# Moving 15 gathered rows from the last stretch of a PEER layer to its projections

## What is computed

```python
proj = rms_norm(x, norm_mix) @ w_in                # q, k, v, u_g, v_g
y = concat(rms_norm(stick_breaking_attention(q, k, v)), rms_norm(chunked_spatial_gating(u_g, v_g)))
x = x + y @ w_out
h2 = rms_norm(x, norm_ffn)
# PEER: product-key retrieval, 8 heads x 16 experts of 16384 for every token
q = rms_norm((h2 @ w_query).reshape(t, 8, 256)); s1, s2 = q halves @ sub_keys
expert_idx, gate = top 16 of the 16 x 16 sums of the two top-16 lists
u_sel = expert_u[expert_idx]                       # (t, 128, 2048)
act = gelu(einsum('tkd,td->tk', u_sel, h2)) * gate
x = x + einsum('tk,tkd->td', act, expert_v[expert_idx])
```

## Time and profile before

| | |
|---|---|
| median of 3 runs | 2982.95 us |
| the profiled execution's own time | 2975.43 us |
| its span, first to last instruction | 2973.7 us |
| busy: PE, DVE, ACT, POOL | 94%, 75%, 40%, 52% |
| mean granted TensorE clock | 0.97 of full speed |
| moved by DMA | 949.46 MB, mean 319 GB/s |
| rows (lines 1328 and 1341) | 208 and 205 instructions |

### The profile page before, as it was taken

How to read it: one execution, slowest core, us unless ns; L and a number is a source line. 1 busy time by engine, 2 the same in 40 slices (tenths; PEclk the granted TensorE clock), 3 DMA queues, 4 the chain that set the end, 5 groups by cost and what they waited for, 6 DMA issues and landing times.

```text
span 2973.7 us, 43212 instructions
## 1 busy us (share of the span) xinstructions
PE 2803.9 (94%) x17757; PEld 2643.4 (89%) x17757; DVE 2233.4 (75%) x3157; ACT 1181.3 (40%) x1387; POOL 1533.8 (52%) x664
## 2 busy tenths in 40 slices
PE   7899899988999989989999899999999999999998
PEld 6677788866879989989999899999999999999997
DVE  6756576766677789979997577777777777778786
ACT  6755532357323333333433333434333333333321
POOL 0000154222242367863334488888867777766662
PEclk9999999989999999999999899999999999999999
DMA  9737638863797868877789899999999999999995
GB/s 362 277 142 263 232 128 328 335 255 127 301 355 279 341 247 297 298 276 298 309 304 371 333 371 353 379 366 383 376 360 407 411 411 388 393 384 382 364 371 217
DMA packets 189485, 949.46 MB, mean 319 GB/s; under 512 B 18352, under 2 KB 77792, under 8 KB 79552
## 3 DMA queue, kind: packets, MB, share of 16 engines
q1 hardware_dynamic: 116704, 485.55, 43.5%
q0 software_dynamic: 60848, 440.59, 38.0%
q10 hardware_dynamic: 11808, 21.70, 1.9%
HBM read 906.46 MB, written 41.22 MB: 319 GB/s over the span
## 4 chain that ended last, share of the span: by engine, by line
PE 69%; DVE 11%; DMA 11%; ACT 5%; POOL 2%; issue 1%; SPq 1%; ACTq 0%; DVEq 0%
PE ps L1686 14%; PE ps L2034 8%; PE ps L2036 8%; PE ps L2035 8%; PE ps L1967 7%; PE ps L1965 6%; PE ps L1966 6%; PE ps L1950 4%; DVE ring_lo L1099 4%; PE ps L1673 4%; DMA ring_raw<-peer_v 3%; POOL ring_lo L617 2%; DVE ps L1341 2%; ACT ring_hi L689 2%; DVE hot_a L1535 2%
## 5 line engine op out<-in xcount | busy, mean ns | idle before, releaser
L617 POOL TENSOR_TENSOR ring_lo<-ring_raw,ring_hi 128x2048 fp32r<-128x2048 f32 x215 | 1000.1, 4652 | 701.5 <-ACT ring_hi L689 699.9
L689 ACT ACTIVATE ring_hi<-ring_raw 128x2048 fp32r<-128x2048 f32 x400 | 762.0, 1918 | 688.2 <-DMA ring_raw<-peer_u 222.8
L1965 PE MATMUL ps<-bT_hi,ring_hi 128*128 128x304 f32 x2048 | 629.3, 307 | 33.0 <-DVE ring_lo L1099 24.8
L2034 PE MATMUL ps<-a_hi,ring_hi 128*128 128x304 f32 x2048 | 629.3, 307 | 31.2 <-DVE ring_lo L1099 15.8
L2036 PE MATMUL ps<-a_hi,ring_lo 128*128 128x304 f32 x2048 | 624.7, 305 | 0.0
L1967 PE MATMUL ps<-bT_hi,ring_lo 128*128 128x304 f32 x2048 | 624.2, 305 | 0.0
L1966 PE MATMUL ps<-bT_lo,ring_hi 128*128 128x304 f32 x2048 | 623.3, 304 | 0.0
L2035 PE MATMUL ps<-a_lo,ring_hi 128*128 128x304 f32 x2048 | 621.8, 304 | 0.0
L1099 DVE TENSOR_TENSOR ring_lo<-ring_raw,ring_hi 128x2048 fp32r<-128x2048 f32 x185 | 452.6, 2462 | 174.9 <-ACT ring_hi L689 174.7
L1965 PEld LDWEIGHTS ps<-bT_hi,ring_hi 128*128 128x128 f32 x2048 | 392.5, 192 | 35.3 <-issue 30.2
L2034 PEld LDWEIGHTS ps<-a_hi,ring_hi 128*128 128x128 f32 x2048 | 390.8, 191 | 36.8 <-issue 27.2
(11 more groups left out here) (310 smaller groups left out, 3772.3 us busy)
## 6 DMA issues: line engine op xcount, KB each, us to landing
ring_raw<-peer_u SPq DMA_DIRECT2D x128, 1024.0 KB, 7.6
ring_raw<-peer_v SPq DMA_DIRECT2D x128, 1024.0 KB, 8.0
ring_raw<-w_in SPq DMA_DIRECT2D x80, 1024.0 KB, 5.4
ring_raw<-w_out SPq DMA_DIRECT2D x32, 1024.0 KB, 4.8
ring_raw<-w_query SPq DMA_DIRECT2D x32, 1024.0 KB, 6.5
g_pair<-gates_scratch SPq DMA_DIRECT2D x64, 320.0 KB, 8.8
gelu_scratch<-ahead ACTq DMA_DIRECT2D x72, 152.0 KB, 5.3
g_in<-gelu_scratch SPq DMA_DIRECT2D x72, 152.0 KB, 7.5
```

The source lines that it names most:

```text
L617: pool.tensor_tensor(ring_lo[s][:], ring_raw[s][:], ring_hi[s][:].bitcast(F32), ALU.subtract)\
L689: act.activation(ring_hi[place(n)][:], ring_raw[place(n)][:], ACT.Copy).then_inc(hi_ok[SLOT[n]], 1)
L1965: pe.matmul(dst, hi[:, e], bT_hi[:, k, 0:NEAR], start=(k == 0), stop=False)
L2034: pe.matmul(dst, hi[:, col], a_hi[:, par, e, :], start=(e == 0), stop=False)
```

## The change

Only the numbers in `fill_rows` change. Beside pieces 94, 98, 102, 106 and 110 of w_in, 115, 119 and 123 of w_out and 130, 132, 134, 136, 138, 140 and 142 of w_query DVE does one row more: two beside each piece of w_in and w_out up to 125, three beside every second piece of w_query. By AHEAD 120 rows are placed instead of 105. The numbers of AHEAD and DOWN stay, so their rows are others: each place there has the row 15 further on in the list. BOTH has 152 rows in place of 167, spread evenly over its 112 pieces (a pattern of 1, 1, 2 in place of 1, 2). Buffers, and which rows read h from SBUF, follow from the same functions.

```diff
 def fill_rows():
     for n in range(92, OUT_B):
-        ROWS_AT[n] = 1 if n % 4 == 2 else 2
+        ROWS_AT[n] = 2
     ROWS_AT[OUT_B - 1] += sum(ATTEND_ROWS)
     for n in range(OUT_B, AHEAD - 1):
-        ROWS_AT[n] = 0 if n == QUERY_B - 1 else 1 if n == QUERY_B - 2 or n % 4 == 3 and n < QUERY_B else 2
+        ROWS_AT[n] = 0 if n == QUERY_B - 1 else 1 if n == QUERY_B - 2 else 3 if n > QUERY_B and n % 2 == 0 else 2
     for t in range(3):
```

## The result

The changed kernel takes **2994.0 us** (median of 12 runs, 2983.16 to 3002.32) beside 2982.32 us of the kernel before on the same chip (12 runs, 2966.58 to 2997.83): a ratio of 1.0039, 95% interval 1.0023 to 1.0056. It is slower by 12 us, where 6.5 us less was forecast. The profiled execution took 2993.33 us (span 2991.6, granted clock 0.971), so it stands for the median; that of before lay 7.5 us under the median that the forecast started from.

What follows compares the result with a forecast made beforehand. PE was taken to bound the kernel nearly everywhere, the last stretch losing some 41 us. Terms -22 - 7.5 + 6.5 - 5 + 10 + 5 + 5 + 1.5 = -6.5 us took 2982.95 to 2976.5; range 2958 to 3000.

Steps and rivals of the forecast that it cites:

- the price of the rows in the projections: w_in, w_out and w_query: the added rows cost +10, +5 and +5 us, 20 together.
- The gates in DOWN: Gates' multiplications move from pieces 230 and 260 to one-row pieces 216 and 245: -5 us (bounds -6.5 and 0).
- The last stretch (-22): BOTH: 15 fewer rows lower the DMA load; three of four PE waits for DVE's `lo` go, -22 us (0 to -30).
- collisions come back: Rival: DVE's and POOL's `lo`s meet at other places, three of four events remain or come anew; 2995 us, chance 0.22.
- The store (-7.5 and +6.5): First tile's store moves from piece 287 to 274: -7.5 us in BOTH, +6.5 in DOWN (bounds 3 to 9).
- w_in (+10): Two late rows, where two buffers serve, cost one more gather round, +10 us (3 to 14); three early rows nothing.
- w_out (+5): Three rows ahead of `hi` and `lo` of 118, 122 and 126 delay them beyond their cover: +5 us (0 to 10).
- w_query (+5): Five rows just fit two pieces; one more row on the end chain, 2.2 us, plus DVE's lag, 0 to 8: +5.
- Retrieval (+1.5): 15 u rows become slower, dependent v rows while DVE is the bound: +1.5 us (ends 0.9 and 3.5).
- the projections saturate: Rival: w_query's DMA demand makes weight loads late and PE stall; cost 35 instead of 20 us, 2991 us, chance 0.08.

Runs made afterwards that it cites:

- last_15_out: Kernel before with 15 of the 16 v3 rows left out, so 152 rows in the last stretch: 2953.15 us beside 2984.6 (0.9907).
- two_on_u: Kernel before, same 167 rows in BOTH, the two-row places on the u pieces from first to last: 2955.84 us beside 2985.84 (0.9905).
- two_on_v: Kernel before, same 167 rows in BOTH, the two-row places on the v pieces from first to last: 3012.42 us beside 2985.84 (1.0104).
- two_before_pool: Kernel before, all 167 rows kept, laid in BOTH by fours of pieces as 1, 2, 2, 1: 2971.49 us beside 2982.81 (0.996).
- w_query_only: Kernel before with only the seven rows of w_query moved, 160 rows left in the last stretch: 2972.02 us (0.9961).

## Why the prediction was wrong, step by step

The step that failed is the price of the rows in the projections: +20 us stood in the sum (+10, +5 and +5), and 37.8 us were measured, since the forecast put the slack behind each place too high and left out the slow clock behind PE's waits. The gates in DOWN, -5 in the forecast and +0.3 measured, and a late input there, 3.3 us, came on top. The last stretch came out near its forecast, for a reason that was in part wrong.

- **The last stretch (-22): the size right, the reason incomplete.** All four waits went, not three, and BOTH with its store gave 31.5 us where 29.5 stood. (The profile of before is a short one in BOTH; reckoned from the medians, BOTH gave about 37.) The prediction put it down to load, and took the undisturbed window of the earlier trace rows, 2230 to 2330, as proof: "the same order of steps loses nothing at even higher load". That reading was wrong. That window lies in the half with two rows on u pieces and the four events in the half with two on v pieces: not the same order. The load on a late transfer was also put too high: with 0.13 of a row less for each piece of 6.65 us, 13.76 us have 0.28 of a row less, 0.7 us at 400 GB/s, not half a row and 1.3 us. Load does count: the changed kernel still has two rows ahead of 12 of DVE's 28 `lo`s in BOTH (14 before), and none of them collides; with its bytes reduced and the formula kept, last_15_out had none either. The rival "collisions come back" was right that order matters; this order had no event. New in BOTH are small stalls at pieces 301 to 329, 6.6 us together.
- **The store (-7.5 and +6.5): both right, one neighbour missed.** Where it left, 7.5 us went; where it arrives, it costs 6.3 us at pieces 276 and 277. POOL and then PE in the changed kernel, the counterpart of the earlier trace rows:

```profile
2132.24 0.60 POOL L638 DMA_DIRECT2D y<-rows  x1
2137.87 0.99 POOL L655 DMA_INDIRECT rows<-peer_u_rows,idx  x1 [5.03 <-DMA y<-rows]
2138.89 4.53 POOL L617 TENSOR_TENSOR ring_lo<-ring_raw,ring_hi 128x2048 fp32r<-128x2048 f32 x1
```

```profile
2143.55 0.62 PE L2034 MATMUL ps<-a_hi,ring_hi 128*128 128x304 f32 x1 [3.84 <-POOL ring_lo L617]
```

  The wait of 3.84 us behind the stand is just under the 4 to 5 forecast. What was missed stands two pieces earlier, 3.3 us: ACT stands idle for 9.7 us and makes no `hi`, since an input of the near tokens comes late. Timeline of ACT:

```profile
2119.04 0.43 ACT L1026 ACTIVATE ps<-g_in 128x304 f32<-128x304 f32 x1 [9.66 <-DMA g_in<-gelu_scratch]
2119.41 1.90 ACT L689 ACTIVATE ring_hi<-ring_raw 128x2048 fp32r<-128x2048 f32 x1
```

  In the list of rows, the plain loads of "out" and "h" stand just ahead and moved to DOWN with them; that they are what delayed this input was not tried.
- **The gates' multiplications (-5): gone here, come back there.** They were expected to run freely beside pieces with one row. Line 1322 in before and then after (ns, shortest, median, longest):

```profile
L1322 DVE TENSOR_TENSOR a_far<-a_far,gate_far x4: 177/1636/3085, 1273.3 to 1975.2; 128x32 f32<-128x32 f32 x4
```

```profile
L1322 DVE TENSOR_TENSOR a_far<-a_far,gate_far x4: 3289/3876/4000, 1182.1 to 1920.6; 128x32 f32<-128x32 f32 x4
```

  All four now lie behind a `lo` of POOL. PE saved 4.5 us at pieces 230 and 231 and 1.9 at 259 and 260, and lost 3.1 at 216 and 217 and 3.5 at 244 and 245, where v row 96's now is: +0.3 together, nothing gained. (Another 1.4 us of DOWN is spread over small differences.) An operation of 0.2 us takes 3.3 to 4.0 us behind its neighbour on POOL; a new place without a look at that neighbour is no gain.
- **w_in (+10): measured +15.9.** The two late rows cost 6.8 and not 10, the three early ones 6.9 and not nothing. The failed step is "three buffers and DVE idle time; nothing": idle time before `hi` was there, but what it had covered was the lead with which the next stretch begins (3.9 us at piece 105 in before, 0.06 with the three rows). The earlier trace rows in the changed kernel (DVE):

```profile
604.39 0.08 DVE L1328 DVE_READ_ACCUMULATOR2_ANT z_far<- 128x1 f32 x1
610.81 2.29 DVE L1328 CUSTOM_DVE_ANT_0 rows<-rows,h_far 128x2048 f32<-128x2048 f32 x1 [6.34 <-DMA rows<-peer_u_rows,idx_far]
...
614.19 2.29 DVE L1099 TENSOR_TENSOR ring_lo<-ring_raw,ring_hi 128x2048 fp32r<-128x2048 f32 x1
```

  Also missed: a late row delays the `lo` that DVE has in its order behind it. So the price is not one round at the end but PE waits before pieces 106 to 109 (10.6 us, four times), and the slow clock behind them.
- **w_out (+5): measured +10.0**, at the places named (118, 122, 126). PE waited 7.4 us in three waits there. The forecast had 1.3 and twice 2 to 3, 5.3 to 7.3 together, and took a value below that; and it left out the slow clock behind a wait (1.5 us after the longest, at piece 122), though the last stretch's events were priced with it.
- **w_query (+5): measured +11.9.** "It just fits" (17.9 of 18.5 us) was an average with 0.6 us of reserve. The chain that ended last of the changed kernel, its counterpart of the earlier trace rows:

```profile
1079.89 6.25 DVE rows L1328
1086.14 0.02 DVE z_far L1328
1086.16 0.26 issue
1086.42 2.75 POOL rows L647
1089.17 0.30 issue
1089.48 9.38 DMA rows<-peer_u_rows,idx_far
```

Then comes a last row of 2.29 us. The earlier trace rows has one gather and one blocked row in this place; here a blocked row (6.25), a slowed issue (2.75) and a gather (9.38) come one after the other, 19 us, because the last row waits for the buffer that the blocked one held. Piece 143, with the scores behind it, lasted 27.28 us in place of 22.07, and the other 6.7 us are waits inside the stretch, at pieces 134 to 141. The forecast allowed 2.2 us for the row and 0 to 8 for what DVE falls behind, and took the lower half.
- **Retrieval (+1.5): -0.4**, no difference that can be read.

Sum by the steps: -31.5 + 6.3 + 3.3 + 0.3 + 1.4 + 15.9 + 10.0 + 11.9 - 0.4 = +17.2, against 17.9 between the spans. The forecast failed in three terms of one kind, the projections: 38 us in place of 20, and by 5 us in the gates. The rival that had the right sign there ("the projections saturate", 15 us more, chance 0.08) was given as a matter of DMA bandwidth; the DMA share in w_query was 0.86 (937.9 to 1081.6), so the saturation was not there, and the mechanism was the round of a buffer. The range, 2958 to 3000, held the time, and the rival nearest to it (2995) is one whose mechanism did not occur: that the two agree is luck.

## What to carry to other kernels

Price an added step in a stretch that is bound elsewhere by the slack of what stands behind it at each place, not by its idle time: the first rows take the slack, the next ones the delay, and a wait of some us costs the slow clock on top (in before the granted clock is 0.51, the lower of TensorE's two levels, 1.2 GHz, from 2656.8 to 2660.0, behind a wait of 4.43 us). Where two engines shut each other out, look at what releases both; where the second row of a step stands was worth 57 us here, and its order alone gave as much as leaving fifteen rows out. Ahead of moving work off a stretch, try another order of it in its place.

## What the runs showed of the hardware

- DVE and POOL, each with two SBUF tiles as input: with POOL's start 0.15 to 0.18 us behind DVE's, DVE's instruction takes 6.8 to 6.95 us in place of 2.28 and POOL's 4.5 to 4.6 as usual; of the 24 long ones in before, two_on_u, two_on_v and two_before_pool 19 are of this kind. In two more DVE was 0.32 and 0.41 us ahead (7.0 and 7.09 us), and in three POOL was first.
- It can also go the other way. In the 17 traces DVE's and POOL's `lo` start within half a microsecond of each other 63 times with POOL not clearly first. 44 times DVE's is the long one; in all 44 POOL's `lo` follows its own gather's issue within 0.02 us. 19 times DVE takes 2.28 and POOL 6.3 to 6.8 us; in 16 of them POOL had stood for 0.04 us or more. With POOL's start more than 0.5 us behind, DVE was never held. The changed kernel has three of these near meetings, and POOL pays in all of them. So the starts in a trace, when they lie this close, do not tell who was first to ask.
- The Trainium skill (SBUF — State Buffer, Who interferes with whom) has the first to issue win. The traces agree where the starts are more than 0.5 us apart; nearer, a start 0.17 us ahead neither shows nor refutes it, so the prediction made too much of that row.
- A gather's issue on POOL that begins while DVE's `lo` runs ends 0.81 to 0.88 us behind it, in each of 79 cases behind 1850: at 2651.09 in two_on_u it takes 2.27 us in place of 0.94, and DVE's `lo` its usual 2.28.
- A row whose second input is in SBUF is blocked in the same way: 6.25 us in the chain above and 5.15 us in w_query_only, 2.29 otherwise.
- A gather's issue on POOL takes 2.75 us when it starts beside such an operation of DVE, 0.94 alone, and in w_in that falls on every second one. It was in the rounds of the prediction, but not in the tail.
